# A two-layer transformer trunk on one core: the first modulations by quarters of the contraction, in step with the weight rows of the first two blocks

## The reference

```python
c_act = silu(c)
mod = c_act @ ada_w[i] + ada_b[i]                 # 6 x 1024 numbers per layer
sh1, sc1, g1, sh2, sc2, g2 = split(mod, 6)
h = rms_norm(x, norm_mix_g[i]) * (1 + sc1) + sh1
y = gla_mixer(h, ...)                             # h @ w_in: q, k (512 each), v, r (1024 each), 16 gate columns
x = x + g1 * y
```

## Time and profile before

| | us |
|---|---|
| median of 3 runs (649.7 to 651.06) | 650.53 |
| the profiled execution | 651.25 |
| its span, first to last instruction | 649.5 |
| TensorE busy | 621.5 (96%) |
| VectorE busy | 474.5 (73%) |
| ScalarE busy | 341.0 (53%) |
| mean granted clock of TensorE | 0.983 |

### The profile page before, as it was taken

How to read it: one execution, slowest core, us unless ns; L and a number is a source line. 1 busy time by engine, 2 the same in 40 slices (tenths; PEclk the granted TensorE clock), 3 DMA queues, 4 the chain that set the end, 5 groups by cost and what they waited for, 6 DMA issues and landing times.

```text
span 649.5 us, 9093 instructions
## 1 busy us (share of the span) xinstructions
PE 621.5 (96%) x3391; PEld 516.6 (80%) x3391; DVE 474.5 (73%) x660; ACT 341.0 (53%) x581; POOL 39.4 (6%) x65
## 2 busy tenths in 40 slices
PE   4699999899999999999999989999999999999997
PEld 2467875677889988998977767788788899899885
DVE  4638998889768978888986777956886555555455
ACT  3437632658645344534458657666854543454440
POOL 3030021000000110111100000000000000000000
PEclk9599999999999999999999989999999999999999
DMA  8999499667588998999964644533476555555501
GB/s 287 387 359 391 164 329 381 219 250 257 190 279 322 373 364 306 360 347 355 364 240 160 208 152 147 178 112 121 157 245 225 186 187 193 194 194 194 192 1 65
DMA packets 59084, 156.43 MB, mean 241 GB/s; under 512 B 2818, under 2 KB 3312, under 8 KB 59056
## 3 DMA queue, kind: packets, MB, share of 16 engines
q1 hardware_dynamic: 47296, 112.41, 49.2%
q0 software_dynamic: 11760, 43.67, 18.9%
HBM read 155.02 MB, written 1.05 MB: 240 GB/s over the span
## 4 chain that ended last, share of the span: by engine, by line
PE 78%; DVE 12%; ACT 4%; issue 3%; DMA 2%; SPq 0%; DVEq 0%; ACTq 0%
PE ps L503 13%; PE ps L504 13%; PE ps L505 13%; PE ps L700 7%; PE ps L699 7%; PE ps L698 7%; PE ps L510 3%; PE ps L512 3%; PE ps L511 3%; DVE w_lo L1433 2%; DMA arena<-in_ada_w_dram 2%; DVE spare L1433 1%; PE ps L607 1%; DVE ada_acc L1450 1%; PE ps L615 1%
## 5 line engine op out<-in xcount | busy, mean ns | idle before, releaser
L1051 ACT ACTIVATE w_hi<-w_raw 128x1024 fp32r<-128x1024 f32 x180 | 189.1, 1058 | 215.4 <-PE ps L505 117.7
L1433 DVE TENSOR_TENSOR w_lo<-w_raw,w_hi 128x1024 fp32r<-128x1024 f32 x180 | 218.3, 1222 | 109.5 <-ACT w_hi L1051 109.3
L700 PE MATMUL ps<-a_hi,w_lo 128*128 128x256 f32 x384 | 108.7, 283 | 0.0
L699 PE MATMUL ps<-a_lo,w_hi 128*128 128x256 f32 x384 | 108.7, 283 | 0.0
L698 PE MATMUL ps<-a_hi,w_hi 128*128 128x256 f32 x384 | 108.6, 283 | 0.0
L503 PE MATMUL ps<-w_hi,m_hi 128*128 128x512 f32 x256 | 100.4, 392 | 0.0
L504 PE MATMUL ps<-w_lo,m_hi 128*128 128x512 f32 x256 | 99.8, 390 | 0.0
L505 PE MATMUL ps<-w_hi,m_lo 128*128 128x512 f32 x256 | 99.7, 389 | 0.0
L503 PE MATMUL ps<-w_hi,a_hi 128*128 128x512 f32 x224 | 93.0, 415 | 5.1 <-DVE a_lo L1587 5.1
L504 PE MATMUL ps<-w_lo,a_hi 128*128 128x512 f32 x224 | 88.6, 396 | 0.0
L505 PE MATMUL ps<-w_hi,a_lo 128*128 128x512 f32 x224 | 88.6, 396 | 0.0
(11 more groups left out here) (202 smaller groups left out, 712.6 us busy)
## 6 DMA issues: line engine op xcount, KB each, us to landing
w_raw<-in_mlp_w_dram SPq DMA_DIRECT2D x64, 1024.0 KB, 5.6
ada_raw<-in_ada_w_dram POOLq DMA_DIRECT2D x40, 1024.0 KB, 7.0
w_raw<-in_gla_w_in_dram SPq DMA_DIRECT2D x12, 1024.0 KB, 13.4
w_raw<-in_moba_w_in_dram SPq DMA_DIRECT2D x12, 1024.0 KB, 7.1
ada_raw<-in_ada_w_dram SPq DMA_DIRECT2D x4, 1024.0 KB, 13.0
arena<-in_ada_w_dram SPq DMA_DIRECT2D x4, 1024.0 KB, 14.2
w_raw<-in_gla_w_out_dram SPq DMA_DIRECT2D x4, 1024.0 KB, 9.0
w_raw<-in_moba_w_out_dram SPq DMA_DIRECT2D x4, 1024.0 KB, 4.8
```

The source lines that it names most:

```text
L699: mm(o, w_hi[:, u, w], a_lo[:, a, :], start=False, stop=False)
L700: z = mm(o, w_lo[:, u, w], a_hi[:, a, :], start=False, stop=u == 3 and k == 1)
L1051: A(dst, w_raw[:, c // 2, c % 2], ACT.Copy).then_inc(hi_made, 1)
L1433: V.tensor_tensor(out, w_raw[:, c // 2, c % 2], w.bitcast(F32), ALU.subtract).then_inc(lo_made, 1)
```

## The change

The first modulations now come and are summed by quarters. Quarter `q` holds the shift and the scale of chunks 2q and 2q + 1 over the whole contraction: two loads of 1 MB, 256 columns of 1024 rows each. SP's order is: `x`, quarter 0, piece 0, quarter 1, piece 1, quarter 2, piece 2, quarter 3 (after the sums of quarter 0), piece 3. Each of these four pieces is 256 whole weight rows over the columns of the first two blocks, so a unit is one chunk for both blocks: 12 matmuls as before, six for block 0 and six for block 1. `ada_rows(q)` sums all eight chunks of a quarter at once. TensorE does quarter 0 before the first unit, and each later quarter `q` so: sums after unit 2q - 2, columns in the middle of unit 2q - 1. The transposes of chunks 4 to 7 move behind unit 2, `glr` stands after unit 6 and `logits` after unit 7, the last. Block 0 and block 1 are both complete after unit 7. `first_mods` makes shift and scale of two chunks. `angles` is cut into three parts, which DVE does after quarter 0's columns wait and after quarters 0 and 1. POOL waits for three quarters before the gate's weights and for four before the first pairs, both together.

```diff
-    FIRST = [(0, 0), (0, 1), (1, 0), (1, 1), (0, 2), (0, 3), (1, 2), (1, 3)]
-    FIRST_DONE = [6, 8]
...
-        ada_pre = [area((4 + 2 * i) * K1, KC // 2, COLS) for i in range(4)]
+        def quarter(q):
+            if q in (1, 2):
+                return area(4 * q * K1, 2, KC, 2 * P)
+            return ada_raw.rearrange("p s k (a n) -> p s (k a) n", a=2)
...
+        ROW_BANK, COL_BANK = (6, 0, 0, 0), (7, 1, 1, 1)
...
+            if v == 0:
+                return (k, 0) if k < 4 else (2 + k % 2, (k - 4) // 2 * SEQ)
             return norm_bank(v) + 2 * (k // 4) + k % 2, ((k % 4) // 2) * SEQ
...
+        def ada_quarter(q, vec):
+            src = ada_w[0, :, vec * D + 2 * q * P:vec * D + 2 * (q + 1) * P]
             return src.rearrange("(k p) n -> p k n", p=P)
...
-            pool.wait_ge(ada_pe, 6)
+            pool.wait_ge(ada_pe, 3)
...
+            pool.wait_ge(ada_pe, 4)
             for s in range(2):
-                pool.wait_ge(ada_pe, 6 + s + 1)
                 load(s)
             nc.gpsimd.dma_start(keep[:, :], keep_d).then_inc(con_in, 16)
...
-            def load_ada(b, half):
-                if b == 3:
-                    sp.wait_ge(ada_pe, half + 1)
-                sp.dma_start(ada_raw[:, half], ada_part(b, half)).then_inc(ada_in[half], 16)
-            def load_pre(i, b):
-                for half in range(2):
-                    sp.dma_start(ada_pre[2 * i + half], ada_part(b, half)).then_inc(ada_pre_in[2 * i + half], 16)
+            def load_quarter(q):
+                if q == 3:
+                    sp.wait_ge(ada_pe, 1)
+                for vec in range(2):
+                    sp.dma_start(quarter(q)[:, vec], ada_quarter(q, vec)).then_inc(quarter_in[q], 16)
...
-            for half in range(2):
-                load_ada(0, half)
-            load_pre(0, 2)
...
-                if l == 0:
-                    order[1:3] = [(1, 0), (0, 1)]
                 for i, (n, d) in enumerate(order):
+                    if l == 0 and i < 4:
+                        load_quarter(i)
+                        load_piece(i, i, w_in[2 * i * P:2 * (i + 1) * P, 0:D])
+                        continue
...
-                    if l == 0 and i == 1:
-                        load_pre(1, 1)
-                        for half in range(2):
-                            load_ada(3, half)
...
+            def ada_rows(q):
+                pe.wait_ge(quarter_in[q], 32)
+                for k in range(KC):
+                    j = 32 * (k % 4)
+                    z = mm(ps[j:j + 1, ROW_BANK[q], :], c_act[:, k:k + 1], quarter(q)[:, :, k, :],
+                           start=k < 4, stop=k >= 4)
                 z.then_inc(ada_pe, 1)
...
+            def ada_cols(q):
+                pe.wait_ge(row_ok, q + 1)
+                for i in range(4):
+                    z = mm(ps[:, COL_BANK[q], i:i + 1], ada_row[:, q % 2, i * P:(i + 1) * P],
                            sel[0:97, :], start=True, stop=True)
                 z.then_inc(col_T, 1)
...
+            def first_turn(group):
+                if group == 1:
+                    pe.wait_ge(a_ok, 2)
+                for tb in range(TB):
+                    pe.wait_ge(xn_ok, tb + 1)
+                    for k in range(4 * group, 4 * group + 4):
+                        bank, at = chunk_at(0, k)
+                        z = tr(ps[:, bank, at + tb * P:at + (tb + 1) * P], xn[:, tb, k * P:(k + 1) * P], eye[:, :])
+                        if tb == TB - 1 and k % 4 >= 2:
+                            z.then_inc(xT_ok, 1)
             def first_norm():
-                for tb in range(TB):
-                    turn_norm(0, tb)
+                first_turn(0)
...
-                for half in range(2):
-                    ada_rows(0, half, 6)
+                ada_rows(0)
                 pe.wait_ge(vec_in, 16 * N_VEC)
                 tr(ps[:, 5, 0:N_ROWS], rows[0:N_ROWS, :], eye[0:N_ROWS, 0:N_ROWS]).then_inc(vec_T, 1)
-                ada_rows(2, 0, 7)
-                pe.wait_ge(pos_cp, 1)
-                ada_cols(0, 4)
-                ada_rows(2, 1, 7)
-                pe.wait_ge(vec_ok, 1)
-                ada_cols(1, 5)
+                ada_cols(0)
...
-                def second_rows(i):
-                    pe.wait_ge(a_ok, 2)
-                    for half in range(2):
-                        ada_rows(ADA_FIRST[i], half, i - 2)
-                def second_cols(i):
-                    ada_cols(i, i - 2)
                 def first_blocks(sides):
-                    for s, (n, u) in enumerate(FIRST):
+                    pe.wait_ge(vec_ok, 1)
+                    pe.wait_ge(pos_cp, 1)
+                    pe.wait_ge(mod_red, 1)
+                    for s in range(KC):
                         pe.wait_ge(lo_made, mix_base[0] + s + 1)
-                        if n == 0:
-                            pe.wait_ge(a_ok, u + 1)
-                        if (n, u) == (0, 2):
-                            pe.wait_ge(mod_red, 4)
-                        for k in range(2):
+                        pe.wait_ge(a_ok, s // 2 + 1)
+                        for n in range(2):
                             for tb in range(TB):
-                                z = three(ps[:, in_bank(n, tb), :], a_hi[:, 2 * u + k, tile(tb)],
-                                          a_lo[:, 2 * u + k, tile(tb)], s % SPLIT, slice(k * COLS, (k + 1) * COLS),
-                                          u == 0 and k == 0, u == 3 and k == 1)
-                            if (s, k) in sides:
-                                sides[s, k]()
-                        z.then_inc(unit_used, 1)
-                        if (s, 2) in sides:
-                            sides[s, 2]()
+                                z = three(ps[:, in_bank(n, tb), :], a_hi[:, s, tile(tb)], a_lo[:, s, tile(tb)],
+                                          s % SPLIT, slice((1 - n) * COLS, (2 - n) * COLS), s == 0, s == KC - 1)
+                            if n == 1:
+                                z.then_inc(unit_used, 1)
+                            if (s, n) in sides:
+                                sides[s, n]()
...
-                pe.wait_ge(mod_red, 2)
-                first_blocks({(0, 2): lambda: second_rows(2), (1, 2): lambda: (second_cols(2), second_rows(3)),
-                              (2, 0): lambda: second_cols(3), (5, 2): glr, (6, 2): logits})
+                first_blocks({(0, 1): lambda: ada_rows(1), (1, 0): lambda: ada_cols(1),
+                              (2, 1): lambda: (first_turn(1), ada_rows(2)), (3, 0): lambda: ada_cols(2),
+                              (4, 1): lambda: ada_rows(3), (5, 0): lambda: ada_cols(3),
+                              (6, 1): glr, (7, 1): logits})
...
-                    act.wait_ge(mod_ok, 2 + v if v else 1 + q // 2)
+                    act.wait_ge(mod_ok, 1 + q)
...
             def ada_out(i):
-                act.wait_ge(ada_pe, 2 * i + 2)
+                act.wait_ge(ada_pe, i + 1)
...
-                for i in range(2):
-                    ada_out(i)
-                for q in range(2):
-                    hi_at(q)
+                for q in range(4):
+                    ada_out(q)
+                    hi_at(2 * q)
                     modulate(0, slice(0, SEQ), 0, (q,))
-                for u in range(2, 4):
-                    hi_at(u)
-                for i in range(2, 4):
-                    ada_out(i)
-                for q in range(2, 4):
-                    modulate(0, slice(0, SEQ), 0, (q,))
-                    hi_at(2 + q)
-                for u in range(6, 8):
-                    hi_at(u)
+                    hi_at(2 * q + 1)
...
-                act.wait_ge(unit_used, FIRST_DONE[n] if l == 0 and n < 2 else mix_base[l] + 4 * n + 4)
+                act.wait_ge(unit_used, KC if l == 0 and n < 2 else mix_base[l] + 4 * n + 4)
...
+            def first_mods(q):
+                two = slice(2 * q, 2 * q + 2)
+                m = modc[:, 0, 0:2, two]
+                dve.wait_ge(col_T, q + 1)
+                V.tensor_tensor(m, ps[:, COL_BANK[q], 0:4].rearrange("p (s k) -> p s k", s=2),
+                                cols[:, C_AB:C_AB + 2 * KC].rearrange("p (s k) -> p s k", s=2)[:, :, two], ALU.add
+                                ).then_inc(mod_red, 1)
+                dve.wait_ge(mod_red, q + 1)
+                m = modc[:, 0, 1, two]
+                g = C_MIX + 2 * q
+                V.scalar_tensor_tensor(m, m, 1.0, cols[:, g:g + 2], op0=ALU.add, op1=ALU.mult).then_inc(mod_ok, 1)
...
-                angles()
+                positions()
...
-                for i in range(2):
-                    first_mods(i, ADA_FIRST[i], 4 + i)
-                modulate(0, slice(0, SEQ), 0, 0, range(2), lo_at)
-                V.memset(restart[:, :, :], 1.0).then_inc(restart_ok, 1)
-                dve.wait_ge(restart_ok, 1)
-                V.memset(restart[:, :, 0:1], 0.0).then_inc(restart_ok, 1)
-                for u in range(2, 4):
-                    lo_at(u)
```

(90 more changed lines are left out.)

14 lines of the change are left out of this document (2 added, 12 removed).

## The result

The changed kernel takes 659.33 us (median of 4 runs, 659.29 to 660.12), the kernel before 650.79 on the same chip (4 runs, 649.7 to 651.08): ratio 1.0146, interval 1.013 to 1.0163. From median to median it is slower by 8.5 us, or 1.3%; the ratio puts it at 1.5%. The forecast was 658.6. The profiled execution took 660.12.

A forecast was written before the change was run, and what follows sets the result against it. The bus was taken to bound the kernel up to 28.88, TensorE's program order after it. The profiled 651.25 plus 8.1 for the late clamp gave 659.35; with the median 0.72 below the profiled run, 658.6, range 652.5 to 664.

The forecast's parts named there:

- The start: First projection matmul on TensorE: forecast at 24.1, 4.8 us earlier than the 28.88 of the kernel before.
- 0.24 us of delay: Load of quarter 0: by the skill's packet cost, 1 KB runs would make it land 0.24 us later.
- Three waits of 1.45: TensorE, between a later quarter's columns and the next pair of chunks: a new wait of 1.45 us, three times.
- the term of 5.33 for the first unit: First unit's 12 matmuls on TensorE: taken to run at the lower clock level, 5.33 us.
- The list of what fills the wait: VectorE during each TensorE wait: addition, scale, odd chunk (0.5), even unit's low part (1.22), low part of the activations.
- The gate chain: Clamp to state updates: clamp at 67.6, 3.4 behind the last of 96 matmuls and 8.1 us late; updates near 94.
- The pairs: POOL's two pairs, issued behind the fourth sums (about 52): VectorE takes them at 59 and 62.6, ahead of the clamp.
- The forecast of 8.1: Clamp in the gate chain: 67.6 against 59.50, 8.1 us late, added whole to the execution time.
- the step that every wait behind 86 is passed on unchanged: Behind 86 us: both engines full, later waits are chains starting at TensorE, so nothing gives the 8.1 us back.
- TensorE's own program order after it: Kernel before: the bus stream bounds it only up to 28.88, TensorE's program order after that.
- The rival in which the clock is up from the first sums: Kernel start: 5.1 us back, 653.5 with the gate chain in front (0.08); with chain slack, faster, 649.1 (0.08).
- The rival of a falling clock: First unit and following sums: clock stays down or falls, 4 to 6 us more, 663 to 665; chance 0.12.

The follow-up runs named there:

- kernel 1: Changed kernel with the sums and columns of each later quarter half a unit earlier; 655.42 us, ratio 1.0089.
- Kernel 2: Changed kernel with ScalarE making the high parts of units 9 and 10 before copying block 0 out of PSUM; 657.61 us, ratio 1.0127.
- kernel 3: Changed kernel with the even unit's high and low weight parts made ahead of the quarter's modulations; 656.99 us, ratio 1.0115.
- kernel 5: Changed kernel with the edits of kernels 1, 2 and 3 together; 655.46 us, ratio 1.0089.
- kernel 9: Kernel 5 with VectorE's first two places for later-modulation steps moved to the end of the first mixer; 660.84 us, ratio 1.0165.
- kernel 11: Kernel 9 with one more place for later-modulation steps moved from ahead of the mask to behind it; 661.99 us, ratio 1.0184.
- kernel 10: Kernel before the change with VectorE's first two places for later-modulation steps moved to the end of the first mixer; 657.81 us, ratio 1.0123.
- Kernel 7: Kernel before the change with 44 unused filler transposes where TensorE waits ahead of the first unit; 651.09 us, ratio 1.002.
- Kernel 6: Changed kernel with 35 unused filler transposes where TensorE waits ahead of the first unit; 656.69 us, ratio 1.0104.
- kernel 4: Changed kernel with the first weight piece loaded ahead of quarter 0 instead of behind it; 662.2 us, ratio 1.0194.
- kernel 8: Changed kernel with the three edits of kernel 5 and the filler transposes of kernel 6; 654.69 us, ratio 1.0077.

## Why the prediction was right

**The start.** 24.1 forecast, 24.22 measured. The landing was 0.2 late (15.12 for 14.9), and the sums and the copy, 4.31 for 4.51, made it up. While only 1 KB runs are on the bus, the windows show 349 GB/s at a share of 1.10, where the kernel before, with 2 KB runs, has 389 and 386:

```profile
18.00:20.00 2.00, 1.64 (x8) 0.76 (x4) 0.26 (x1) 1.22 (x2) 0.00 (x0) 1.00 1.10 349
26.00:28.00 2.00, 2.00 (x7) 1.55 (x6) 1.83 (x5) 0.00 (x0) 0.00 (x0) 1.00 1.10 349
```

So 1 KB runs cost a tenth of the bus, which as an estimate is 0.6 us on the 2 MB of quarter 0, where alone it matters. The landing does not show it: it was at 15.12 here, but at 14.53 to 14.82 in kernels 1, 2, 3, 5, 9 and 11, which load quarter 0 in the same order, against 14.72 before and 14.57 in kernel 10. By the Trainium skill ("DMA: Bandwidth & Descriptors", "Why small descriptors are slow") the estimate was 4.5%, or 0.24 us of delay: the windows show twice the share, and the delay lies within the spread of the landings.

**TensorE's order.** Three waits of 1.45 forecast, 1.43, 1.36 and 1.36 measured. Chunks 2, 4 and 6 were forecast at 36.5, 47.4 and 57.4 and came at 35.87, 46.77 and 56.81; the last matmul at 64.2, measured 63.64; the third block at 65.8, measured 65.18. All are 0.6 early, mainly for one reason: the term of 5.33 for the first unit. It took 4.43 (24.22 to 28.65), since the clock came up inside it (matmuls follow each other by 0.43 up to 27.3, by 0.23 from 27.6 on). Kernel 1 shows that the waits are what was claimed: without them TensorE ends 4.15 earlier. The list of what fills the wait was wrong in one point. VectorE's low part was named; kernel 3 shows that ScalarE's even chunk and `a_hi` set it to within 0.3.

**The gate chain.** The clamp was forecast 3.4 behind the last matmul, and is. Kernel 2 takes 1.5 of it away by ScalarE's order alone. The pairs, forecast to be taken at 59 and 62.6, were taken at 57.78 and 60.91 and cost nothing in the changed kernel, but 2.8 and 0.6 as soon as TensorE is early (kernel 1): they are a second bound, 1 us behind the first.

**What is given back.** Nothing between the updates and 379 us, as forecast (7.54, within 0.3). The forecast of 8.1 was 0.6 too high by the first unit, and 1.2 too low by the longer stretch at the lower clock at 382 us, which it did not have. The two nearly cancel, which is luck: right to 0.7, but the step that every wait behind 86 is passed on unchanged left out the clock. The longer stretch is shown for the profiled execution (660.12) alone; the other three took 659.29 to 659.35.

**What bounds the kernel before.** "TensorE's own program order after it" was too simple. Kernel 7 started TensorE's logits 3.6 earlier and gained 1.1 at the updates, and nothing at the end. TensorE's order, the weight pieces and VectorE's list end within some 1 us of one another at the clamp. So an earlier start was worth about 1 there, while whatever made the logits' end late counted in full. The rival in which the clock is up from the first sums was priced at 5.1 us. Kernel 6 comes near it: 3.8 at the updates, 0.7 of it because its first sums start at 14.43. The clock came up inside its first sums only (2.74 for 16), and the first unit had 1.5 to give instead of 2.4.

**The clock.** The rival of a falling clock did not occur: three waits of 1.4 us, with 9 to 10 us of work before each, left it at 1.00. The Trainium skill ("TensorE: Matmul & The Clock Gate", "HAM oscillation") tells of a kernel whose waits, longer than the work between them, bring the clock down each time. The three waits here are not such a case, and don't speak against it. In the wait of 6.64 in kernel 10 the clock falls to 0.50, and so it does in the wait of 3.33 near 380 us, or up to 1.5 us behind it, in every kernel; there the trace agrees with it.

## What to carry to other kernels

Cutting the first data into finer parts starts the expensive engine earlier, but each part has a chain of small steps of fixed length behind it (here 3.8 to 3.9 us), and if less work than that is in hand, the chain becomes a wait in every round. Before paying for an early start, follow it to the first place where three engines meet, and ask how much slack the others have there: bring the start forward by filler work and see whether the end moves at all. A step moved away from one meeting place pushes back all that stand behind it in the list, so look up the deadline of the last, not only of the first.

## What was not expected of the hardware

- The clock column read 1.00 in 16 to 18 us of the changed kernel, while 16 row sums took 3.59 there and take 1.90 later. Early on, the level is to be read from the paces of known instructions.
- Where the clock first came up was not the same from one profiled execution to another, though the instructions up to there were nearly the same: in the first unit, at 27.3, in the changed kernel; behind it, under the second quarter's sums, in kernel 9; and in kernels 3, 10 and 11 some groups before the first matmul ran at the full clock (the columns in 1.05). This moved the start by 1 to 1.5 us. One execution of each kernel was profiled, so it may differ as much between executions of one kernel: the six of kernel 3 range from 656.3 to 659.36, with a mean clock of 0.989 in the two longest and 0.992 to 0.997 in the others.
- Kernels 1, 3, 5, 6 and 7 have a stretch of 3.4 us at the lower clock just behind the updates that neither the kernel before nor the changed one has. It cost about 1.6 each time and hid part of each gain in these profiles. Windows of kernel 5:

```profile
90.00:92.00 2.00, 2.00 (x9) 1.38 (x7) 1.97 (x3) 0.00 (x0) 0.00 (x0) 0.76 0.99 380
92.00:94.00 2.00, 2.00 (x6) 1.52 (x6) 1.97 (x4) 0.00 (x0) 0.70 (x1) 0.50 1.08 410
94.00:96.00 2.00, 2.00 (x11) 1.17 (x9) 1.95 (x3) 0.99 (x2) 0.00 (x0) 0.89 0.96 270
```

  The changed kernel, with a wait of the same 1.69 before its updates, stays at 1.00, and so do kernels 2, 4 and 8 (1.66 to 1.69). What tips it stays open. So does why the stretch near 380 us was twice as long (6.8 us) in the changed kernel and kernel 4 as in the other twelve (3.4), which costs the changed kernel 1.2 us against these in the profiles.
